# A depthwise convolution's fourth channel tile moved from VectorE to GpSimd

## What is computed

```python
def conformer_branch(z, dw, dw_b, ln_g, ln_b, w_out, grid, horizontal):
    u = z[..., :CONV_DIM] * jax.nn.sigmoid(z[..., CONV_DIM:])
    ...
    y = depthwise_conv(u, dw)        # width 31, one weight per channel and tap
    y = layer_norm(y.reshape(B, T, C) + dw_b, ln_g, ln_b)
    return jax.nn.silu(y) @ w_out
```

## Time and profile before

| | before |
|---|---|
| median of three runs | 4474.88 us |
| lowest and highest | 4465.52, 4477.34 us |
| the profiled execution, its own time | 4475.39 us |
| its span in the profile | 4473.6 us |
| mean granted TensorE clock | 0.963 of full |
| TensorE busy | 94% |
| VectorE busy | 31% |
| ScalarE busy | 24% |
| GpSimd busy | 1% |

### The profile page before, as it was taken

How to read it: one execution, slowest core, us unless ns; L and a number is a source line. 1 busy time by engine, 2 the same in 40 slices (tenths; PEclk the granted TensorE clock), 3 DMA queues, 4 the chain that set the end, 5 groups by cost and what they waited for, 6 DMA issues and landing times. The chain is left out here.

```text
span 4473.6 us, 108758 instructions
## 1 busy us (share of the span) xinstructions
PE 4219.4 (94%) x51156; PEld 2514.7 (56%) x51156; DVE 1365.3 (31%) x2121; ACT 1074.1 (24%) x1778; POOL 58.1 (1%) x52
## 2 busy tenths in 40 slices
PE   7999999988999999999999989999997899999998
PEld 3566666665555555555555556666666344444443
DVE  1555555554730000100000255555554220010000
ACT  2444444442020000100000244444443120010000
POOL 0000000000000000000000000000000000000000
PEclk8999999988999999999999989999998999999999
DMA  5000000003431111111111200000000532222222
GB/s 187 23 8 23 23 22 23 27 20 125 135 124 52 52 49 52 42 52 52 52 52 52 84 23 8 22 21 22 21 31 13 199 111 76 78 68 75 75 80 75
DMA packets 67388, 260.42 MB, mean 58 GB/s; under 512 B 7680, under 2 KB 9984, under 8 KB 66048
## 3 DMA queue, kind: packets, MB, share of 16 engines
q1 hardware_dynamic: 62208, 219.18, 15.4%
q10 hardware_dynamic: 3456, 29.04, 1.6%
q0 software_dynamic: 1280, 5.24, 0.3%
HBM read 239.80 MB, written 13.63 MB: 57 GB/s over the span
## 5 line engine op out<-in xcount | busy, mean ns | idle before, releaser
L584 PE MATMUL psum<-arena,ring 128*128 128x512 f32 (+1 forms) x4992 | 1805.0, 523 | 29.4 <-ACT arena L1326 22.6
L584 PEld LDWEIGHTS psum<-arena,ring 128*128 128x128 f32 x4992 | 950.5, 191 | 890.0 <-issue 816.0
L879 PE MATMUL psum<-arena 32*32 32x32 f32 (+4 forms) x40512 | 835.0, 212 | 147.0 <-issue 112.0
L879 PEld LDWEIGHTS psum<-arena 32*32 32x32 f32 (+3 forms) x40512 | 753.4, 122 | 336.8 <-issue 269.4
L766 PE MATMUL psum<-arena,ring 128*128 128x512 f32 (+1 forms) x1408 | 554.3, 523 | 2.5 <-ACT arena L1419 1.6
L1254 PE MATMUL psum<-arena,ring 128*128 128x512 f32 (+1 forms) x1440 | 520.2, 521 | 0.0
L1254 PEld LDWEIGHTS psum<-arena,ring 128*128 128x128 f32 x1440 | 273.6, 190 | 242.0 <-issue 229.6
L766 PEld LDWEIGHTS psum<-arena,ring 128*128 128x128 f32 x1408 | 254.2, 194 | 201.6 <-issue 178.3
L2161 DVE TENSOR_TENSOR arena<-psum,arena 128x768 f32<-128x768 f32 (+1 forms) x44 | 36.3, 825 | 718.8 <-PE psum L584 718.8
L2102 DVE TENSOR_TENSOR arena<-psum,arena 128x768 f32<-128x768 f32 (+1 forms) x48 | 39.6, 825 | 617.9 <-PE psum L584 617.9
L1698 ACT ACTIVATE arena<-psum 128x768 f32<-128x768 f32 (+1 forms) x44 | 31.0, 704 | 698.8 <-PE psum L584 698.8
(11 more groups left out here) (131 smaller groups left out, 2464.2 us busy)
## 6 DMA issues: line engine op xcount, KB each, us to landing
ring<-w_stream_in SPq DMA_DIRECT2D x408, 512.0 KB, 3.7
x_spill<-arena ACTq DMA_DIRECT2D x2, 3072.0 KB, 8.7
arena<-ya_spill ACTq DMA_DIRECT2D x2, 3072.0 KB, 10.0
arena<-x_spill ACTq DMA_DIRECT2D x2, 3072.0 KB, 18.5
ring<-w_stream_in ACTq DMA_DIRECT2D x8, 512.0 KB, 6.3
arena<-x_in ACTq DMA_DIRECT2D x1, 3072.0 KB, 14.3
arena<-ups_in SPq DMA_DIRECT2D x16, 192.0 KB, 2.4
ya_spill<-arena POOLq DMA_DIRECT2D x8, 384.0 KB, 6.8
```

The lines of the kernel that those rows point to most:

```text
L584: mm = eng.matmul(psum[0:lhs[k].shape[-1], tile, a - off:b - off], lhsT=lhs[k], rhs=rhs[k][:, a:b], start=(k == 0), stop=(k == len(lhs) - ...
L879: return pe.matmul(out, lhsT=lhs, rhs=rhs, start=start, stop=stop, skip_group_check=True)
```

## The change

Tile 3 of the convolution (all its taps, in both layers) is issued by GpSimd. GpSimd has no fused form here, so a tap becomes a multiplication of the whole tile by the tap's weight into a scratch slot (LW), a wait on a new semaphore, and an addition of the shifted scratch to y (two additions in layer 0, one in layer 1). GpSimd begins when VectorE has written u3. On VectorE the place of tile 3's taps is taken by sc, the second modulation third and sm, without taps between them. TensorE's cmean now waits for GpSimd's last tap, and so does VectorE before it centres the convolution (after p00). Tiles 0 to 2 keep their instructions.

```diff
--- before.py
+++ after.py
@@ -292,16 +292,18 @@
     v = []
     for j in range(CT):
         v += [f"u{j}"]
+        if j == CT - 1:
+            v += SC + SM
+            continue
         for n in range(len(conv_taps(l))):
             v += [f"y{j}_{n}"] + [x for x in SIDE[l].get((j, n), []) if x[:3] != "mod"]
     v += [f"{x}{j}" for j in range(CT) for x in ("sp", "uv")]
     v += ["p00"] + [f"cc{j}" for j in range(CT)] + [f"cn{j}" for j in range(CT)] + parts_of_merge()[1:]
-    return dict(PE=[n for n in branch_flow(l) if n[0] != "t" or n[1] == "r"] + merge_flow(), A=a, V=v, G=[n.replace("p", "m") for n in parts_of_merge() if n[1] != "0"])
+    return dict(PE=[n for n in branch_flow(l) if n[0] != "t" or n[1] == "r"] + merge_flow(), A=a, V=v, G=[f"y{CT - 1}_{n}" for n in range(len(conv_taps(l)))] + [n.replace("p", "m") for n in parts_of_merge() if n[1] != "0"])
 
 
 SC, SM = [f"sc{j}" for j in range(CT)], [f"sm{j}" for j in range(CT)]
-SIDE = [{(1, 30): ["mod1"], (3, 16): SC, (3, 20): ["mod2"], (3, 27): SM},
-        {(2, 14): ["mod4"], (3, 14): SC + ["mod5"] + SM}]
+SIDE = [{(1, 30): ["mod1"]}, {(2, 14): ["mod4"]}]
 
 
 def names_out(per):
@@ -382,6 +384,7 @@
         ups = [sem(f"ups_in_{i}") for i in range(3)]
 
         phases = {}
+        s_weighted = sem("tap_weighted")
 
         def phase(key, names, turns=1, chunks=()):
             ph = {e: Steps(sem(f"{key}_{e}"), ns, turns) for e, ns in names.items() if ns}
@@ -595,6 +598,43 @@
 
         def load_chunk(eng, n):
             eng.dma_start(ring[:, None, (n % 4) * BW:(n % 4 + 1) * BW], w_v[:, n:n + 1, :]).then_inc(w_in[n % 4], 16)
+
+        def weighted_count(l, m):
+            return m + (len(conv_taps(0)) - 1) * l
+
+        def conv_tap(eng, S, l, j, m):
+
+
+            c0 = cols(l)
+            o = conv_taps(l)[m]
+            y, u = slot(CY + j), slot(CU + j)
+            if m == 0:
+                eng.tensor_scalar(y[:, c0:T], u[:, c0:T], par_c("dw", j * TAPS + 15), par_c("dwb", j), ALU.mult, ALU.add).then_inc(*S.mark(f"y{j}_0"))
+                return
+            eng.wait_ge(*S.at(f"y{j}_{m - 1}"))
+            w = par_c("dw", j * TAPS + 15 + o)
+            lo, hi = max(0, -o), max(0, o)
+
+            if eng is nc.gpsimd:
+                weighted = slot(LW)
+                eng.tensor_scalar(weighted[:, c0:T], u[:, c0:T], w, None, ALU.mult).then_inc(s_weighted, 1)
+                eng.wait_ge(s_weighted, weighted_count(l, m))
+                u = weighted
+
+            def add(out, in0):
+                if eng is nc.gpsimd:
+                    return eng.tensor_tensor(out, out, in0, ALU.add)
+                return eng.scalar_tensor_tensor(out=out, in0=in0, scalar=w, in1=out, op0=ALU.mult, op1=ALU.add)
+
+            if c0 == 0:
+                add(y[:, lo:CTX - hi], u[:, lo + o:CTX - hi + o])
+            if l % 2 == 0:
+                gy, gu_ = (x[:, CTX:T].rearrange("p (r w) -> p r w", w=GRID_W) for x in (y, u))
+                ins = add(gy[:, :, lo:GRID_W - hi], gu_[:, :, lo + o:GRID_W - hi + o])
+            else:
+                a, b, s = CTX + lo * GRID_W, T - hi * GRID_W, o * GRID_W
+                ins = add(y[:, a:b], u[:, a + s:b + s])
+            ins.then_inc(*S.mark(f"y{j}_{m}"))
 
         hs = [slot(H0 + j) for j in range(KT)]
         cond = arena[:, COND:COND + KT * 32].rearrange("p (k m) -> p k m", m=32)
@@ -1213,7 +1253,7 @@
                 for name in merge_flow():
                     if name == "cmean":
                         pe.wait_ge(*modr.at(mod_thirds(l)[-1], 1))
-                        pe.wait_ge(*V.at(f"y{CT - 1}_{len(conv_taps(l)) - 1}"))
+                        pe.wait_ge(*G.at(f"y{CT - 1}_{len(conv_taps(l)) - 1}"))
                         mm = project(pe, 3, [ones] * CT, cv, c0, c0)
                     elif name == "cvar":
                         pe.wait_ge(*V.at(f"cc{CT - 1}"))
@@ -2059,27 +2099,6 @@
                 taps = conv_taps(l)
                 tiles = branch_tiles(l)
 
-                def grid(k, t, horizontal=True):
-                    return slot(k, CTX).rearrange("p (r w) -> p r w", w=GRID_W)
-
-                def tap(j, o, m):
-
-                    w = par_c("dw", j * TAPS + 15 + o)
-                    lo, hi = max(0, -o), max(0, o)
-                    ins = None
-                    if c0 == 0:
-                        ins = dve.scalar_tensor_tensor(out=slot(CY + j, lo, CTX - hi), in0=slot(CU + j, lo + o, CTX - hi + o),
-                                                       scalar=w, in1=slot(CY + j, lo, CTX - hi), op0=ALU.mult, op1=ALU.add)
-                    if l % 2 == 0:
-                        y, u = grid(CY + j, 0), grid(CU + j, 0)
-                        ins = dve.scalar_tensor_tensor(out=y[:, :, lo:GRID_W - hi], in0=u[:, :, lo + o:GRID_W - hi + o],
-                                                       scalar=w, in1=y[:, :, lo:GRID_W - hi], op0=ALU.mult, op1=ALU.add)
-                    else:
-                        a, b, s = CTX + lo * GRID_W, T - hi * GRID_W, o * GRID_W
-                        ins = dve.scalar_tensor_tensor(out=slot(CY + j, a, b), in0=slot(CU + j, a + s, b + s),
-                                                       scalar=w, in1=slot(CY + j, a, b), op0=ALU.mult, op1=ALU.add)
-                    return ins
-
                 def centred(name, tile, dst):
                     dve.wait_ge(*PE.at(name))
                     for j in range(CT):
@@ -2106,20 +2125,15 @@
                     dve.wait_ge(*PE.at(f"ca{j}"))
                     dve.tensor_tensor(slot(CU + j, c0), psum[:, 0, 0:n], slot(G0 + j % 2, c0), ALU.mult).then_inc(*V.mark(f"u{j}"))
                     dve.wait_ge(*V.at(f"u{j}"))
-                    for m, o in enumerate(taps):
-                        if m == 0:
-                            dve.tensor_scalar(slot(CY + j, c0), slot(CU + j, c0), par_c("dw", j * TAPS + 15), par_c("dwb", j),
-                                              ALU.mult, ALU.add).then_inc(*V.mark(f"y{j}_0"))
-                        else:
-                            dve.wait_ge(*V.at(f"y{j}_{m - 1}"))
-                            tap(j, o, m).then_inc(*V.mark(f"y{j}_{m}"))
-                        for name in SIDE[l].get((j, m), []):
-                            if name == "sc0":
-                                centred("smean", tiles["smean"], SV)
-                            elif name == "sm0":
-                                scaled("sm", "sr", SV, G0 + 2)
-                            elif name[:3] == "mod":
-                                mod_ready(int(name[3]))
+                    if j == CT - 1:
+                        centred("smean", tiles["smean"], SV)
+                        mod_ready(mod_thirds(l)[1])
+                        scaled("sm", "sr", SV, G0 + 2)
+                        continue
+                    for m in range(len(taps)):
+                        conv_tap(dve, V, l, j, m)
+                        if (j, m) in SIDE[l]:
+                            mod_ready(mod_thirds(l)[0])
                 for j in range(CT):
                     dve.wait_ge(*PE.at(f"sp{j}"))
                     if j == 0:
@@ -2132,6 +2146,7 @@
                 if l == 0:
                     mod_ready(3)
                 part("p00")
+                dve.wait_ge(*G.at(f"y{CT - 1}_{len(taps) - 1}"))
                 centred("cmean", 3, CY)
                 scaled("cn", "cr", CY, NT)
                 for name in parts_of_merge()[1:]:
@@ -2196,6 +2211,9 @@
                 ph = phases[f"branch{l}"]
                 V, G = ph["V"], ph["G"]
                 c0 = cols(l)
+                pool.wait_ge(*V.at(f"u{CT - 1}"))
+                for m in range(len(conv_taps(l))):
+                    conv_tap(pool, G, l, CT - 1, m)
                 before = {}
                 for name in parts_of_merge():
                     b, q = int(name[1]), int(name[2])
```

## The result

The changed kernel took 4501.82 us, the median of five runs (4496.09 to 4514.32), against 4474.88 us before (five runs). The ratio is 1.0061 with a 95% interval of 1.0048 to 1.0074: slower, by 21 to 33 us. The profiled execution is the slowest of the five, 4514.32 us.

What follows compares the result with a forecast made beforehand. TensorE, busy 94%, was taken to bound the kernel. GpSimd's terms for tile 3 in layer 0 put its end at 1323.1, so cmean waits 8.6 us, plus 1.5 of clock: +10.1, 4485 against the median; range 4470 to 4507.

Steps and rivals of the forecast that it cites:

- the removal: VectorE, both layers: taking tile 3's taps off it was costed at 0, bounds -0.8 and 0 us.
- the forecast of +10 us inside the noise: cmean, layer 0: 8.6 us of waiting and 1.5 of clock, +10.1 us, inside the 13.4 us a measurement can tell.
- GpSimd becomes the bound: Rival at cmean's wait, layer 0: multiplication costs what the addition does, +27.6 to +31.4 us, 4503 to 4506; chance 0.22.
- the middle: GpSimd's multiplication, layer 0: 1.24 us, between VectorE's same operation at 679 ns and GpSimd's own addition at 1804 ns.
- borders of 0.96 and 1.35: GpSimd's 31 multiplications, layer 0: a mean outside these microseconds would show the forecast wrong.
- 60 additions, with their overlap: GpSimd, layer 0: 55.1 us for 20,880 columns and 60 fixed costs, less 2.0 us where two additions overlap.
- hand-overs: GpSimd's waits on itself, layer 0: two a tap at 0.20 us, 12.0 us, and 0.2 for the first.
- collisions: Layer 0, VectorE's eight two-input sm and uv instructions beside GpSimd: 3.8 us, half of 7.6.
- The shared door: Rival, layer 0: VectorE's eight two-input instructions each hold GpSimd up for their length, 7.6 us, total +13.9; chance 0.20.
- Hidden altogether: Rival, layer 0: multiplication near VectorE's 0.68 us, last tap before cmean, time 4474 to 4475; chance 0.20.
- break-even: Layer 0: a multiplication of 0.96 us, the point that decides whether GpSimd's last tap ends before cmean.
- The clock: TensorE's cmean, layer 0: after the wait it runs partly at 1.2 instead of 2.4 GHz, adding 1.5 us.

Runs made afterwards that it cites:

- the column of ones: Changed kernel, with GpSimd's tap multiplication given a second operation, times a column of ones: ratio 0.9994 to the kernel before.
- fast form: Changed kernel, with GpSimd taking tile 0 in place of tile 3 and multiplying in two operations, the second times an immediate 1.0: ratio 1.0005 to the kernel before.
- slow one: Changed kernel, with GpSimd taking tile 0 in place of tile 3 and keeping the one-operation multiplication: ratio 0.9987 to the kernel before.

## Why the prediction was right in part and wrong in its forecast

**Right: what bounds.** TensorE does, VectorE's taps were hidden, and the removal was worth nothing that can be measured. The three kernels with a two-operation multiplication, where a tile is off VectorE and nothing is late, are 0.9994 to 1.0005 of before, with intervals that reach 0.1 to 0.2% to either side. sm moved up by 4.9 us against u3 (some 5 predicted). The transposes went from 5.93 to 5.55 us (5.62 in the timeline), but TensorE reached cmean 98.9 us behind u3 as before.

**Right: the place.** The loss sits in one wait, cmean in layer 0; layer 1 was hidden, with 28.7 us to spare (28 to 35 were worked out). GpSimd's merge additions, said not to be touched, shift with the rest (the first from 1351.99 to 1384.40) and cost nothing of their own.

**Wrong: the forecast of +10 us inside the noise.** Measured was +27, within 2 us of the rival "GpSimd becomes the bound" (4503 to 4506), to which I gave 0.22; the range held it. The step that failed is the multiplication of 1.24 us, "the middle" between two rows. It took 2.20 us alone and 2.28 in the mean, outside both ends (0.68 and 1.80) and outside the borders of 0.96 and 1.35 that were named as the sign of being wrong. From u3 to the last addition, layer 0 took 126.0 us where I had 107.5:

| term | predicted | measured |
|---|---|---|
| centre tap | 1.24 | 0.97 |
| 30 multiplications | 37.2 | 68.3 |
| 60 additions, with their overlap | 53.1 | 51.1 |
| hand-overs | 12.2 | 5.6 |
| collisions | 3.8 | 2.6, contained in the terms above |

The multiplications are 31.1 us over. The hand-overs are 6.6 under: GpSimd waits for itself 0.07 to 0.11 us each time, not the 0.20 of the earlier trace rows, which is an order from another engine. The additions, worked out from the earlier trace rows, were right within 4%. Collisions: the two long multiplications are 1.37 and 0.81 us over 2.20, an addition pair beside uv about 0.4, sm 4.85 us in place of 3.56. That is about 2.6 us for GpSimd against the 3.8 and against the 7.6 of the rival "The shared door", which is set aside as a cause.

That the rival and the range met the time is luck. The rival has 125.0 us for the same stretch, 1.0 short. Its multiplications of 1.80 us are 14.2 too low in all, and that is made up by terms that are too high: 6.6 in the hand-overs, 3.8 of collisions counted beside the other terms, 2.0 in the additions and 0.8 in the centre tap. The upper end of the range rests on the same sum.

**Wrong: the upper end of the multiplication.** I took GpSimd's own addition, with two inputs, as the most that one input could cost. The bound had a reason, but no row. The two-operation form lies inside the bounds, at 0.91 us, and with it the rival "Hidden altogether" would have been right. Its break-even of 0.96 was too strict, as it holds the hand-overs of 12 us: the mean with the column of ones was 1.10 us, and the last tap was still 7 us early.

**The clock.** I had 1.5 us for it and it was 2.35, after a wait of 27.2 us in place of 8.6. The runs give a row of it: cmean took 1.79 us over its 5.32 after a wait of 11.5, and 2.94 after one of 30.2.

## What to carry to other kernels

Move work to a slower engine only with a deadline in hand: the time from its input to its first reader, divided by the number of steps. Here it was 3.19 us a tap, and 4.06 missed it (126.0 / 31) while 2.89 did not (89.7 / 31). On GpSimd, don't price an operation by its neighbours; time one instance of the very form, and try a tensor_scalar with a second, neutral operation. No run here tried the fused form of the tap on GpSimd, so how it would compare is open. And where nothing waits for VectorE, relieving it is worth nothing by itself.

## What was not expected of the hardware

- **One operation costs more than two.** A GpSimd tensor_scalar in float32 on 128 partitions takes 2.20 and 1.56 us for 768 and 512 columns with one operation, 0.905 and 0.69 with two: (2.20 - 1.56) / 256 = 2.5 ns a column against 0.84. The Trainium skill, page "GPSIMD Engine Reference", section "Engine selection", has one-input operations there at roughly line rate, at the 1.2 GHz of its "Specifications" 0.83 ns a column. The two-operation form agrees with that; the one-operation form is three times off. Why the form with one operation is slow is not shown by these runs; they exclude place, destination, multiplication or addition, and immediate or column.
- **VectorE pays for a busy GpSimd.** Taps with both inputs in the arena took 65.6 us in place of 33.2 beside GpSimd's fast form, 50.7 beside its slow one. Instructions with one input from PSUM did not change: sc took 3.55 us with GpSimd at work, as in the earlier trace rows, and each sp 0.94 to 0.96 us. The Trainium skill, page "SBUF — State Buffer", section "Who interferes with whom", says that two-SBUF-input instructions of VectorE contend with reading ones of GpSimd, and that an instruction with at most one SBUF input does not, outside the modes that use both ports. Both agree with these traces. VectorE's centre tap, whose one tile lies in the arena, was lengthened all the same, from 0.68 to 1.63 us beside the fast form and to 1.06 and 1.22 beside the slow one; whether it runs in such a mode is not shown.
- **The two engines do not shut each other out for whole instructions.** The same section of the Trainium skill calls the shared ports an exclusive lock. In the 65.6 us beside the fast form VectorE did 33.2 us of work and GpSimd 20 taps, which I estimate at 51 us undisturbed (20 x 0.905 us, and 33 for their additions in the timeline of the changed kernel). That is 84 us of work in 65.6, so the times of the profile overlap in part. A GpSimd instruction met by VectorE's was longer by up to 1.4 us.
- **A tensor_tensor with a broadcast column** is cheaper on GpSimd (1.04 us for 512 columns) than one with two full tiles (1.26).
